# Spreading the activation sums over two plain pairs, with five plain pairs in the first network

## What is computed

```python
def swiglu(h, w1, w3, w2):
    return (jax.nn.silu(h @ w1) * (h @ w3)) @ w2

h = rmsnorm(x, g_ffn1[l])
x = x + 0.5 * swiglu(h, w1_a[l], w3_a[l], w2_a[l])     # network one
...                                                    # attention part
h = rmsnorm(x, g_ffn2[l])
x = x + 0.5 * swiglu(h, w1_b[l], w3_b[l], w2_b[l])     # network two
```

## Time and profile before

| | before |
|---|---|
| time, median of 3 runs | 1153.97 us (1153.1 to 1154.5) |
| profiled execution: time | 1153.61 us |
| its span, first to last instruction | 1151.8 us |
| mean granted TensorE clock | 0.982 of 2.4 GHz |
| TensorE, matmuls | 1113.0 us busy (97%), 6058 instructions |
| VectorE | 774.1 us busy (67%) |
| ScalarE | 543.4 us busy (47%) |
| DMA | 28.1% of 16 engines, 102.99 MB |

### The profile page before, as it was taken

One profiled execution on the slowest core, in us unless ns is written; L12 is line 12 of the kernel. 1 busy time (PEld: TensorE's weight loads), 2 busy tenths in 40 slices (PEclk: granted clock), 3 DMA queues, 4 the chain that ended last, 5 costly groups with the idle time before them and its releaser, 6 DMA issues.

```text
span 1151.8 us, 15666 instructions
## 1 busy us (share of the span) xinstructions
PE 1113.0 (97%) x6058; PEld 953.9 (83%) x6066; DVE 774.1 (67%) x1085; ACT 543.4 (47%) x874; POOL 0.2 (0%) x4
## 2 busy tenths in 40 slices
PE   7799999999999999998899999999899999999996
PEld 6689899988998788887677788888798899989985
DVE  6866378845878778677575555666785478637854
ACT  6544155523653456666555433323553256424641
POOL 0000000000000000000000000000000000000000
PEclk9999999999999999998899999999999999999998
DMA  8133233332324212111020123433233232333221
GB/s 283 56 110 92 92 111 107 98 108 92 99 72 123 84 44 66 46 55 41 33 73 28 38 87 94 140 105 95 74 104 99 92 111 96 98 100 110 80 68 74
DMA packets 32904, 102.99 MB, mean 89 GB/s; under 512 B 4160, under 2 KB 5568, under 8 KB 32832
## 3 DMA queue, kind: packets, MB, share of 16 engines
q1 hardware_dynamic: 32832, 102.01, 28.1%
HBM read 99.90 MB, written 2.10 MB: 89 GB/s over the span
## 4 chain that ended last, share of the span: by engine, by line
PE 84%; DVE 9%; ACT 4%; issue 3%; DMA 0%; DVEq 0%; SPq 0%; ACTq 0%
PE acc_pair L1177 24%; PE acc_pair L1179 23%; PE acc_pair L1178 23%; PE pair_bank L1177 2%; PE pair_bank L1178 2%; PE pair_bank L1179 2%; DVE w_lo L762 2%; PE bank L1177 1%; PE bank L1179 1%; PE bank L1178 1%; ACT w_hi L474 1%; ACT rope L632 1%; DVE t_lo L815 1%; PE bank L1185 1%; DVE rstd L787 1%
## 5 line engine op out<-in xcount | busy, mean ns | idle before, releaser
L1177 PE MATMUL acc_pair<-xg_hi,w_hi 128*128 128x512 f32 (+1 forms) x684 | 265.7, 388 | 7.2 <-DVE w_lo L992 7.2
L1178 PE MATMUL acc_pair<-xg_lo,w_hi 128*128 128x512 f32 (+1 forms) x684 | 259.8, 380 | 0.0
L1179 PE MATMUL acc_pair<-xg_hi,w_lo 128*128 128x512 f32 (+1 forms) x684 | 258.6, 378 | 0.0
L474 ACT ACTIVATE w_hi<-w_raw 128x1024 fp32r<-128x1024 f32 (+2 forms) x158 | 152.6, 975 | 152.0 <-PE acc_pair L1179 151.9
L762 DVE TENSOR_TENSOR w_lo<-w_raw,w_hi 128x1024 fp32r<-128x1024 f32 (+2 forms) x158 | 177.5, 1125 | 47.2 <-ACT w_hi L474 46.5
L1177 PEld LDWEIGHTS acc_pair<-xg_hi,w_hi 128*128 128x128 f32 x684 | 131.9, 193 | 29.9 <-issue 8.4
L1179 PEld LDWEIGHTS acc_pair<-xg_hi,w_lo 128*128 128x128 f32 x684 | 131.2, 192 | 25.0
L1178 PEld LDWEIGHTS acc_pair<-xg_lo,w_hi 128*128 128x128 f32 x684 | 132.1, 193 | 20.2 <-issue 0.7
L1179 PE MATMUL acc_pair<-hid_hi,w_lo 128*128 128x512 f32 x352 | 138.8, 394 | 0.0
L1178 PE MATMUL acc_pair<-hid_lo,w_hi 128*128 128x512 f32 x352 | 138.2, 393 | 0.0
L1177 PE MATMUL acc_pair<-hid_hi,w_hi 128*128 128x512 f32 x352 | 136.9, 389 | 0.0
(11 more groups left out here) (217 smaller groups left out, 2092.8 us busy)
## 6 DMA issues: line engine op xcount, KB each, us to landing
w_raw<-in_w13b SPq DMA_DIRECT2D x44, 512.0 KB, 3.6
w_raw<-in_w13a SPq DMA_DIRECT2D x40, 512.0 KB, 3.6
w_raw<-in_wmix SPq DMA_DIRECT2D x22, 512.0 KB, 3.5
w_raw<-in_w2a SPq DMA_DIRECT2D x16, 512.0 KB, 3.6
w_raw<-in_w2b SPq DMA_DIRECT2D x16, 512.0 KB, 3.6
w_raw<-in_wgate SPq DMA_DIRECT2D x8, 512.0 KB, 3.5
w_raw<-in_wend SPq DMA_DIRECT2D x8, 512.0 KB, 3.5
w_raw<-in_wo SPq DMA_DIRECT2D x8, 512.0 KB, 3.6
```

What stands on the lines that cost most here:

```text
L474: act.activation(w_hi[:, s, 0:width], w_raw[:, s, 0:width], ACT.Copy).then_inc(whi_done, 1)
L1177: pe.matmul(o, w_h, r_h, start=first, stop=False, skip_group_check=check)
L1178: pe.matmul(o, w_h, r_l, start=False, stop=False, skip_group_check=check)
L1179: return pe.matmul(o, w_l, r_h, start=False, stop=last, skip_group_check=check)
```

## The change

The first network gets five plain pairs (and 17 fast ones), the second keeps four. The rounds of activation sums are spread: rounds 0 and 1 stand in plain pair `PLAIN - 3`, round 2 in plain pair `PLAIN - 2`. In network one that is pairs 2 and 3, in network two pairs 1 and 2. Within the first of them ScalarE now makes both rounds' `xgf` before both `t_hi`, and VectorE both rounds' `tsum` before both `t_lo`. `xgf` and `tsum` move from the room of `hid_hi` and `hid_lo` to that of `s_hi` and `s_lo`. The fast pairs' numbers are counted anew, so that in network two they begin at 17 and not at 18.

```diff
-PLAIN = 4
-FAST = NF - PLAIN
+PLAIN = (5, 4)
...
-            with ExitStack() as start:
-                unused_hi = sb("unused_hi", [P, PLAIN, SEQ], F32, start)
-                xgf = sb("xgf", [P, 2, 2, SEQ], F32, start)
-                unused_lo = sb("unused_lo", [P, PLAIN, SEQ], F32, start)
-                tsum = sb("tsum", [P, 2, 4, HALF], F32, start)
...
             s_raw = sb("s_raw", [P, 4, QW], F32, ffn)
+            with ExitStack() as start:
+                xgf = sb("xgf", [P, 2, 2, SEQ], F32, start)
+                tsum = sb("tsum", [P, 2, 4, HALF], F32, start)
             s_hi = sb("s_hi", [P, 2, 4, QW], F32R, ffn)
...
-                        return b * FAST + f - PLAIN
+                        return b * (NF - PLAIN[0]) + f - PLAIN[b]
...
-            def sums_operands(b):
-
-                def gained(q):
+            def sums_operands(b, qs):
+
+                for q in qs:
+                    if q >= 2:
+                        act.wait_ge(tsum_done, 4 * (Q * b + q - 1))
                     for i, m in enumerate((q, Q + q)):
                         act.activation(xgf[:, q % 2, i, :], x[:, m, :], ACT.Copy,
                                        scale=gains[:, 2 * b, m:m + 1]).then_inc(xgf_done, 1)
-
-                gained(0)
-                for q in range(Q):
-                    if q + 1 < Q:
-                        if q:
-                            act.wait_ge(tsum_done, 4 * (Q * b + q))
-                        gained(q + 1)
+                for q in qs:
                     act.wait_ge(tsum_done, 4 * (Q * b + q + 1))
                     act.activation(t_hi[:, :, q, :], tsum[:, q % 2], ACT.Copy).then_inc(t_hi_done, 1)
...
-                for j in range(PLAIN):
+                b = n_norm // 2
+                for j in range(PLAIN[b]):
                     u = base + 2 * j
-                    if j == PLAIN - 1:
+                    if j == PLAIN[b] - 1:
...
-                    if j == PLAIN - 2:
-                        sums_operands(n_norm // 2)
+                    if j == PLAIN[b] - 3:
+                        sums_operands(b, (0, 1))
+                    elif j == PLAIN[b] - 2:
+                        sums_operands(b, (2,))
...
-                sums(0)
-                for q in range(Q):
-                    if q + 1 < Q:
-                        sums(q + 1)
+                for q in qs:
+                    sums(q)
+                for q in qs:
                     n = Q * b + q
...
-                pe.wait_ge(t_lo_done, Q * (1 + g // FAST))
+                pe.wait_ge(t_lo_done, Q * (1 if u < MIX else 2))
...
-                        for j in range(RING, 2 * PLAIN):
-                            if j == 2 * PLAIN - 1:
-                                first_product(u + 2 * PLAIN)
+                        for j in range(RING, 2 * lo):
+                            if j == 2 * lo - 1:
+                                first_product(u + 2 * lo)
                             unit(u + j, 0, xg, K8)
```

More of the change, by code:

```diff
@@ L400, in fast_index @@
                     f = f0 + (u0 - chunk_base(base, c)) // 2
-                    if f0 <= f < f0 + n and u0 >= chunk_base(base, c) and f >= PLAIN:
-                        return b * FAST + f - PLAIN
+                    if f0 <= f < f0 + n and u0 >= chunk_base(base, c) and f >= PLAIN[b]:
+                        return b * (NF - PLAIN[0]) + f - PLAIN[b]
             return None
@@ L585, in ffn @@
                     if c == 0:
-                        lo = PLAIN
+                        lo = PLAIN[n_norm // 2]
                         plain_pairs(u, fb, n_norm)
```

## The result

| | before | after |
|---|---|---|
| time, median on record | 1154.01 us (4 runs) | 1142.31 us (4 runs, 1136.11 to 1142.89) |
| ratio | | 0.9885, 95% interval 0.9854 to 0.9915 |
| median of the executions with a recorded clock, over all experiments | 1153.41 us (41) | 1141.58 us (16, 1135.88 to 1145.18) |
| profiled execution: time, span | 1153.61, 1151.8 us | 1136.11, 1134.3 us |
| mean granted TensorE clock, that execution | 0.982 | 0.995 |

The change is faster by 1.15%, 11.7 us.

What follows compares the result with a forecast made beforehand. TensorE, busy 1113.0 of 1151.8 us, was taken to bound the kernel, with waits on w_lo to be won. 1153.61 less 4.16 (network one) and 4.54 (network two) gave 1144.9 us, range 1142.5 to 1147.5.

Steps and rivals of the forecast that it cites:

- the two places: TensorE's waits on w_lo(8) before each network's first fast pair, 5.84 and 2.67 us, set by VectorE's sums standing ahead.
- The scratch's room: New place of xgf and tsum: no new wait, no cost unless VectorE were slower there.
- The renumbering and the transfers: s_hi parity and accumulator slots change, free times do not; unit 10's weights released some 19 us before use: no cost.
- the clock after the remaining wait: Network one, after the remaining wait of about 1.9 us: clock falls to 1.2 GHz, costing 1.60 us; gain 4.16 us.
- rival 1: Network one's clock holds after the remaining wait, gain there 5.76 us; 1143.3 us, chance 0.30.
- Rivals 3 and 4: 3: network one's wait stays 5.84 us, 1149.7 us, chance 0.05; 4: unit 10's transfer lands late, 1156.9 us, chance 0.01.
- rival 4: Network one: unit 10's weight transfer takes 30 us and lands late, slower than before; 1156.9 us, chance 0.01.
- Rival 2: A further short wait in network two or clock fall in the attention part; 1145.9 to 1146.6, both some 1148 us; chance 0.14.

Runs made afterwards that it cites:

- five_only: Kernel before with only the fifth plain pair of network one added, all three rounds of sums together; 1147.22 us, ratio 0.9952 to the kernel before.
- two_together: Changed kernel with network two's three rounds of sums together in pair 2, as before the change; 1147.26 us, ratio 0.9948 to the kernel before.
- old_room: Changed kernel with xgf and tsum back in their old room, that of hid_hi and hid_lo; 1140.95 us, ratio 0.9903 to the kernel before.
- again: Changed kernel run once more with no edit; 1138.51 us, ratio 0.9890 to the kernel before.
- shift8: Changed kernel with eight extra unused matmuls of 512 columns near network one's end, delaying the attention part 1.8 us; 1140.90 us, ratio 0.9897 to the kernel before.
- pad2b: Changed kernel with two idle VectorE additions of 512 columns ahead of w_lo(10) in network one, second sample; 1144.97 us, ratio 0.9935 to the kernel before.
- spread_only: Changed kernel with four plain pairs in both networks, so the spreading of the sums alone; 1146.50 us, ratio 0.9954 to the kernel before.

## Why the prediction came out as it did

**What bounds the kernel, and the two places.** Right. Both waits on w_lo L762 were the DVE program's order, and they went as worked out: first product 61.44 for 61.53, fast pair 68.07 for 68.15; network two 4.51 us for 4.54, with 0.9 us of slack for 0.8.

**The parts.** Five_only and two_together bear out the split by network: the fifth pair carries network one, the spreading network two. In network one the spreading was to give 0.5 us; five_only's wait is longer by 0.3 to 0.8 us. The scratch's room costs nothing that shows (old_room). The renumbering and the transfers never appeared in a wait.

**The step that failed: the clock after the remaining wait.** The term of the sum that failed is the 1.60 us of slow matmuls. I took the fall to 1.2 GHz for the forecast, at a chance of 0.50 against 0.30 for rival 1, because three of four waits between 1.5 and 2.7 us in the trace before were followed by one. Two of those lie in the attention part, where TensorE is less dense and other idle time stands near them, and one was longer than what was left. At the place itself the study has seven waits of 1.53 to 2.02 us, and the clock fell after two (again, old_room), and not in the profile of the change itself, where it stayed at 1.00; after nine waits of 2.31 to 5.84 us it fell eight times (not after five_only's 2.32 in network two). The size was right: where the clock fell, first product to fast pair took 8.26 us (again, 69.72 - 61.46), and 6.63 where it held. So the likeliest case was rival 1, 1143.3 us, and the median is 1.0 below it on record, 1.7 over all executions. The Trainium skill's rule that the prediction set beside this (page "TensorE: Matmul & The Clock Gate", section "HAM oscillation — how this bites in real kernels") gave rival 1, and the five waits of 1.53 to 2.02 us without a fall agree with it; the two falls after 2.01 and 2.02 us and the seven after 2.31 to 2.77 us do not.

**The rest below the range.** Rival 1's 1143.3 less some luck was to hold it at 1142.5. I gave the attention part's clock 0.8 us downwards, as if one profile stood for it. Its lost clock runs from 1.7 to 10.2 us among the thirteen profiles, and the changed kernel's executions span 9.3 us. The medians differ in lost clock by 18.4 - 12.5 = 5.9 us; networks one and two account for 5.1 of it (three falls), of which the changed kernel keeps 0.5 (two falls of 1.7 us in seven profiles). The remainder, 1.3 us of lost clock or 1.1 us of time, is about what rival 1 was too high by (1.0 or 1.7 us). It is rough, since the end of the span, where a low clock costs next to nothing, varies by 1.9 us among the profiles. Whether it is chance or belongs to the change is not settled: shift8 and pad2b were to tell, and neither did beyond its spread. That the kernel before is so much steadier (29 of its 41 executions lie between 1152.62 and 1154.93 us) and the changed one is not, I can't explain.

**Rivals 3 and 4** did not come: w_lo(10) was ready where worked out, not 5.84 us late, and no wait of TensorE's in the networks was released by a transfer. (The 1156.9 us of rival 4 is off by its own terms: w_hi(10) 11.2 us late, at 70.4 instead of 59.2, would give 1144.9 + 11.2 = 1156.1.)

**Rival 2** did not come either: network two's slack held, and no profile of the changed kernel lost more in the attention part than the kernel before.

## What to carry to other kernels

A long wait of the bounding engine costs twice, by its length and by the slow matmuls after it; shortening it to 1.53 to 2.02 us here won both in five of seven profiles. Before a wait is priced, follow the program of the engine that ends it: in network two the sums cost TensorE nothing once they stood ahead of a read that had to wait for TensorE anyway, while in spread_only the same order in network one opened a wait of 2.44 us. And where the clock falls by chance, take the size of an effect from many executions with their clocks, not from the profiled one, and give the range that spread.

## What was not expected of the hardware

- The changed kernel lost between 5.7 and 16 us of clock (0.995 to 0.986 of 1134 to 1143 us), of which some 4 to 6 us lie at the end of the span, where next to no matmul runs; the rest are single falls to 1.2 GHz, 1.7 us of lost clock each in the profiles. Its time followed at 0.86 us for each us lost (16 executions of one program).
- A fall that comes ahead of a further wait costs less than its length: in spread_only unit 6 ran slow after 45.09 and the first product still started only 0.4 us later than in the kernel before. Likewise, how early TensorE came through its start changed the wait (1.53, 2.01, 2.02 us in three profiles of one program) and the time of the first product by 0.3 us at most (61.44, 61.17, 61.46).
